# Attention: the turning of the probabilities in two 64-row halves of the array

## The reference

```python
def _sink_attend(q, k, v, mask, sink):
    s = jnp.einsum('bqhgd,bkhd->bhgqk', q, k) * (HEAD_DIM ** -0.5)
    if mask is not None:
        s = jnp.where(mask, s, -jnp.inf)
    m = jnp.maximum(jnp.max(s, axis=-1), sk)          # sk: a logit per head
    p = jnp.exp(s - m[..., None])
    den = jnp.sum(p, axis=-1) + jnp.exp(sk - m)
    o = jnp.einsum('bhgqk,bkhd->bqhgd', p, v)
    return o / den
# latent: blocks of 128 queries; keys are 256 cached ones + a window of 128 before, own 128, 128 after
```

## Time and profile before

| | us |
|---|---|
| median of 3 runs (lowest, highest) | 2705.36 (2704.15, 2711.06) |
| span of the profiled execution (no other time of it is recorded) | 2702.7 |
| attention: from the first scores to the last tile's turning | 173.9 to 1056.5 |
| PE busy over the span | 2641.0 (98%) |
| DVE, ACT, POOL busy | 1248.0 (46%), 870.3 (32%), 641.9 (24%) |
| L1173 (turning), busy on PE | 167.9, 1264 instructions |
| L1190 (values), busy on PE | 168.0, 2528 instructions |

### The profile page before, as it was taken

One profiled execution on the slowest core, in us unless ns is written; L12 is line 12 of the kernel. 1 busy time (PEld: TensorE's weight loads), 2 busy tenths in 40 slices (PEclk: granted clock), 3 DMA queues, 4 the chain that ended last, 5 costly groups with the idle time before them and its releaser, 6 DMA issues.

```text
span 2702.7 us, 47576 instructions
## 1 busy us (share of the span) xinstructions
PE 2641.0 (98%) x17435; PEld 2315.5 (86%) x17435; DVE 1248.0 (46%) x3286; ACT 870.3 (32%) x2222; POOL 641.9 (24%) x833
## 2 busy tenths in 40 slices
PE   5899999999999999999999999999999999999998
PEld 3688888888888887787899999999999999999787
DVE  3656657475665647554234251424233341425533
ACT  3434526353452535222213131222223131313211
POOL 2522031222203121333003030312213040403332
PEclk9999999999999999999999999999999999999999
DMA  9512030211203032443122041313222030315543
GB/s 357 205 49 76 10 95 14 64 56 49 74 12 95 13 93 102 140 135 103 36 36 84 17 83 42 76 42 61 65 38 82 19 108 16 84 43 148 170 140 109
DMA packets 187800, 219.26 MB, mean 81 GB/s; under 512 B 27248, under 2 KB 132480, under 8 KB 185680
## 3 DMA queue, kind: packets, MB, share of 16 engines
q1 hardware_dynamic: 177616, 189.11, 24.8%
q10 hardware_dynamic: 9984, 27.37, 2.6%
HBM read 178.27 MB, written 38.17 MB: 80 GB/s over the span
## 4 chain that ended last, share of the span: by engine, by line
PE 90%; DVE 3%; DMA 2%; issue 2%; ACT 1%; POOL 1%; SPq 0%; ACTq 0%; DVEq 0%; POOLq 0%
PE psum L521 18%; PE psum L523 17%; PE psum L522 17%; PE psum L1190 5%; PE psum L1173 5%; PE psum L1157 2%; PE psum L1160 2%; PE psum L2390 2%; PE psum L2455 2%; PE psum L1940 2%; PE psum L1942 2%; PE psum L1941 2%; PE psum L2458 2%; PE psum L1475 2%; PE psum L1476 2%; PE psum L1477 2%
## 5 line engine op out<-in xcount | busy, mean ns | idle before, releaser
L521 PE MATMUL psum<-h_hi,m_w_lo 128*128 128x384 f32 (+1 forms) x1600 | 594.0, 371 | 1.1 <-ACT gt_nat L1388 1.1
L523 PE MATMUL psum<-h_hi,m_w_hi 128*128 128x384 f32 (+1 forms) x1600 | 573.6, 359 | 0.0
L522 PE MATMUL psum<-h_lo,m_w_hi 128*128 128x384 f32 (+1 forms) x1600 | 573.1, 358 | 0.0
L523 PEld LDWEIGHTS psum<-h_hi,m_w_hi 128*128 128x128 f32 x1600 | 300.5, 188 | 27.0
L521 PEld LDWEIGHTS psum<-h_hi,m_w_lo 128*128 128x128 f32 x1600 | 301.3, 188 | 26.0 <-issue 1.6
L522 PEld LDWEIGHTS psum<-h_lo,m_w_hi 128*128 128x128 f32 x1600 | 301.6, 189 | 22.4
L521 PE MATMUL psum<-h_hi,attn_w_lo 128*128 128x384 f32 (+1 forms) x800 | 291.7, 365 | 0.9 <-DVE attn_w_lo L506 0.6
L523 PE MATMUL psum<-h_hi,attn_w_hi 128*128 128x384 f32 (+1 forms) x800 | 285.8, 357 | 0.0
L522 PE MATMUL psum<-h_lo,attn_w_hi 128*128 128x384 f32 (+1 forms) x800 | 285.5, 357 | 0.0
L881 ACT ACTIVATE arena<-arena,stats 128x640 f32<-128x640 f32 (+2 forms) x272 | 216.1, 795 | 143.3 <-DVE stats L964 143.3
L964 DVE CUSTOM_DVE_ANT_0 arena<-psum,wmask,stats 128x640 f32<-128x640 f32 (+2 forms) x256 | 206.1, 840 | 56.7 <-PE psum L1160 52.9
(11 more groups left out here) (318 smaller groups left out, 4671.9 us busy)
## 6 DMA issues: line engine op xcount, KB each, us to landing
m_bc<-gate_rows_mlstm SPq DMA_DIRECT2D x128, 256.0 KB, 3.4
m_w_raw<-in_mlstm_w_in SPq DMA_DIRECT2D x40, 512.0 KB, 4.7
h_full<-gated_output SPq DMA_DIRECT2D x29, 512.0 KB, 4.1
gated_output<-gT SPq DMA_DIRECT2D x8, 1088.0 KB, 5.2
layer_output<-xb_out ACTq DMA_DIRECT2D x17, 512.0 KB, 2.7
h_hi_full<-layer_output SPq DMA_DIRECT2D x17, 512.0 KB, 4.8
out<-h_hi_full ACTq DMA_DIRECT2D x17, 512.0 KB, 5.0
xb<-in_x_sample ACTq DMA_DIRECT2D x16, 512.0 KB, 7.0
```

The source lines that it names most:

```text
L521: pe.matmul(out, self.lo[:, k, :], E.h_hi[:, k, tok], start=(k == 0), stop=False)
L522: pe.matmul(out, self.hi[:, k, :], E.h_lo[:, k, tok], start=False, stop=False)
L523: ins = pe.matmul(out, self.hi[:, k, :], E.h_hi[:, k, tok], start=False, stop=(k == KT - 1))
```

## The change

The transposes are cut by query rows. Each 128x128 tile becomes two of 64 rows by 128 columns, each against a 64x64 identity, one in rows 0 to 63 of the array and one in rows 64 to 127. The ten tiles of a block (five of each head, in one row of slots, head 0 first) lie in three banks: slots 0 to 7 have their lower query half in bank 4 and the upper in bank 5, and slots 8 and 9 have both halves in bank 7. The upper halves are taken in another order (slots 8 and 9 first), so that both halves of the array are never in bank 7 together; a new semaphore `s_upper` guards that. ACT copies slots 0 to 7 from banks 4 and 5 in one instruction of 1024 columns, DVE copies slots 8 and 9 (256 columns) from bank 7, and only for blocks of five tiles. `s_pT` is raised once by two, after the last transpose. `turn` waits once, ahead of its first transpose, for the exponentials of both heads. ACT's copy of block 1 has a new wait for the gate projection's banks, since the buffer is shared with it.

The copy after the two scans has half the columns. The diff:

```diff
--- before.py
+++ after.py
@@ -553,8 +553,8 @@
         shuf = spare[:, 5, 0:512]
         flat = spare[:, :, :].rearrange("p a n -> p (a n)")
         prob = [flat[:, 5 * D + 512 + b * 640:5 * D + 512 + (b + 1) * 640] for b in range(4)]
-        probT = [sb(f"probT{b}", [P, 2, 5, P]) for b in range(2)]
-        gth = [probT[1][:, :, :, :].rearrange("p h t q -> p (h t q)")[:, e * 512:(e + 1) * 512] for e in range(2)]
+        probT = [sb(f"probT{b}", [P, 10, P]) for b in range(2)]
+        gth = [probT[1][:, :, :].rearrange("p t q -> p (t q)")[:, e * 512:(e + 1) * 512] for e in range(2)]
         k_hi = sb("k_hi", [P, KREQ], F32R)
         sink = sb("sink", [P, NHEAD])
         stats = sb("stats", [P, 6, 2, 2])
@@ -562,7 +562,7 @@
         rden = sb("rden", [P, 4, 2, 4])
         rspr = sb("rspr", [P, 2, HD])
         rturned = sb("rturned", [8, P])
-        kvout = probT[0][:, 0, 0, :].rearrange("p (a d) -> p a d", a=2)
+        kvout = probT[0][:, 0, :].rearrange("p (a d) -> p a d", a=2)
 
         J = Projection(E, ctx, "attn", 5, E.first_w)
         s_cs = [sem(f"rotary_loaded{b}") for b in range(2)]
@@ -581,6 +581,7 @@
 
 
 
+        s_upper = sem("upper_halves_of_last_tiles")
         s_rq, s_rt, s_rw, s_rb, s_scaled = (sem(x) for x in (
             "recip_turned", "recip_copied", "recip_stored", "recip_rows_loaded", "o_scaled"))
         NU = 2 * NT
@@ -610,6 +611,20 @@
             if b == CTX:
                 return [VT_REQ]
             return [0, 1] + [VT_LAT + b + x for x in (-1, 0, 1) if 0 <= b + x < NS]
+
+        PAIRED = 8
+        LONG = NS - 2
+
+        def long_before(b):
+
+            return min(max(b - 1, 0), LONG)
+
+        def turned_half(slot, half):
+
+            if slot < PAIRED:
+                return E.bank[4 + half][:, slot * HD:(slot + 1) * HD]
+            at0 = (slot - PAIRED) * P + half * HD
+            return E.bank[7][:, at0:at0 + HD]
 
         def scores_of(w):
 
@@ -860,18 +875,16 @@
                             act.wait_ge(s_sarg, at(bbase + b + 1))
                             act.activation(esink[:, b % 2, :], sarg[:, b % 2, :], ACT.Exp).then_inc(s_es, 1)
 
-                        def turned_second(b):
+                        def turned_pairs(b):
                             act.wait_ge(s_pT, at(base + 2 * b + 2))
                             if b == 0 and sub == 0:
                                 act.wait_ge(s_kvst, at(kv * 32 + 32))
+                            if b == 1:
+                                act.wait_ge(s_release, at(kv * NB + NG * (3 + 2 * sub)))
                             act.wait_ge(s_pv, at(bbase + (b - 1 if b >= 2 else 0)))
-                            n = min(4, len(value_tiles(b)))
-                            ins = act.copy(probT[b % 2][:, 1, 0:n, :],
-                                           E.bank[5][:, 0:n * P].rearrange("p (t q) -> p t q", t=n))
-                            if len(value_tiles(b)) == 5:
-                                ins = act.copy(probT[b % 2][:, :, 4, :],
-                                               E.bank[7][:, 0:2 * P].rearrange("p (h q) -> p h q", h=2))
-                            ins.then_inc(s_pTB, 1)
+                            n = min(PAIRED, 2 * len(value_tiles(b)))
+                            act.copy(probT[b % 2][:, 0:n, :].rearrange("p t (a q) -> p t a q", a=2),
+                                     E.PS[:, 4:6, 0:n * HD].rearrange("p a (t q) -> p t a q", q=HD)).then_inc(s_pTB, 1)
 
                         def exponential(b, hh):
                             w = 2 * b + hh
@@ -903,7 +916,7 @@
                                 act.copy(E.w_hi[:, 1, :], spare[:, 1, :]).then_inc(s_ewhi, 1)
                             if 2 <= s < NT:
                                 exponential(s, 0)
-                            turned_second(s - 1)
+                            turned_pairs(s - 1)
                             if 2 <= s < NT:
                                 exponential(s, 1)
                                 sink_exp(s)
@@ -966,14 +979,13 @@
                                                      op0=ALU.add, op1=ALU.min,
                                                      accum_out=negm[:, b % 2, hh:hh + 1]).then_inc(s_nm, 1)
 
-                        def turned_first(b):
-                            dve.wait_ge(s_pT, at(base + 2 * b + 1))
+                        def turned_rest(b):
+                            if len(value_tiles(b)) < 5:
+                                return
+                            dve.wait_ge(s_pT, at(base + 2 * b + 2))
                             dve.wait_ge(s_pv, at(bbase + (b - 1 if b >= 2 else 0)))
-                            if b == 0 and sub == 0:
-                                dve.wait_ge(s_kvst, at(kv * 32 + 32))
-                            n = min(4, len(value_tiles(b)))
-                            dve.tensor_copy(probT[b % 2][:, 0, 0:n, :],
-                                            E.bank[4][:, 0:n * P].rearrange("p (t q) -> p t q", t=n)).then_inc(s_pTA, 1)
+                            dve.tensor_copy(probT[b % 2][:, PAIRED:10, :],
+                                            E.bank[7][:, 0:2 * P].rearrange("p (t q) -> p t q", t=2)).then_inc(s_pTA, 1)
 
                         def denominators(b):
                             p = b % 2
@@ -1066,7 +1078,7 @@
                                 softmax_max(2 * s)
                                 softmax_max(2 * s + 1)
                             if s < NT + 1:
-                                turned_first(s - 1)
+                                turned_rest(s - 1)
                                 denominators(s - 1)
                             if s >= 2:
                                 gate(s - 2)
@@ -1100,7 +1112,7 @@
                         if g == 0 and sub == 0:
                             pe.wait_ge(s_vS, at(kv * 3 + 3))
                         elif g == 0:
-                            pe.wait_ge(s_pTA, at(kv * (2 * NT) + NT))
+                            pe.wait_ge(s_pTA, at(kv * (2 * LONG) + LONG))
                             pe.wait_ge(s_pTB, at(kv * (2 * NT) + NT))
                         elif g == 2 and sub == 0:
                             pe.wait_ge(s_kvo, at(kv * 2 + 2))
@@ -1120,7 +1132,7 @@
                         pe.wait_ge(S.s_hd, NT)
                     pe.wait_ge(s_release, at(kv * NB + NG))
                     pe.wait_ge(s_og, at(kv * (2 * NT)))
-                    pe.wait_ge(s_pTA, at(kv * (2 * NT)))
+                    pe.wait_ge(s_pTA, at(kv * (2 * LONG)))
                     pe.wait_ge(s_pTB, at(kv * (2 * NT)))
                     settle(E, pe)
                     for r, (a, z) in enumerate(VGROUPS):
@@ -1163,15 +1175,22 @@
                                     ins.then_inc(s_S, 1)
 
                     def turn(b):
-                        pe.wait_ge(s_pTA, at(bbase + b))
+                        pe.wait_ge(s_pTA, at((kv * 2 + sub) * LONG + long_before(b)))
                         pe.wait_ge(s_pTB, at(bbase + b))
-                        for hh in range(2):
-                            w = 2 * b + hh
-                            pe.wait_ge(s_p, at(base + w + 1))
-                            for t in range(len(value_tiles(b))):
-                                out = E.bank[4 + hh][:, t * P:(t + 1) * P] if t < 4 else E.bank[7][:, hh * P:(hh + 1) * P]
-                                ins = pe.transpose(out, prob[w % 4][:, t * P:(t + 1) * P], E.ident[:, :])
-                            ins.then_inc(s_pT, 1)
+                        n = len(value_tiles(b))
+                        tiles = [(hh, t) for hh in range(2) for t in range(n)]
+                        low, high = tiles, tiles[PAIRED:] + tiles[:PAIRED]
+                        pe.wait_ge(s_p, at(base + 2 * b + 2))
+                        for i, pair in enumerate(zip(low, high)):
+                            if i == PAIRED:
+                                pe.wait_ge(s_upper, at((kv * 2 + sub) * LONG + long_before(b + 1)))
+                            for half, (hh, t) in enumerate(pair):
+                                r = slice(half * HD, half * HD + HD)
+                                ins = pe.transpose(turned_half(hh * n + t, half), prob[(2 * b + hh) % 4][r, t * P:(t + 1) * P],
+                                                   E.ident[r, r])
+                            if n == 5 and i == 1:
+                                ins.then_inc(s_upper, 1)
+                        ins.then_inc(s_pT, 2)
 
                     def pv(b):
 
@@ -1182,12 +1201,12 @@
                         if b >= LONE:
                             pe.wait_ge(s_rs, at((kv * 2 + sub) * (NT - LONE) + b - LONE + 1))
                             pe.transpose(spread, rspr[:, :, :].rearrange("p h d -> p (h d)"), E.ident[:, :])
-                        pe.wait_ge(s_pTA, at(bbase + b + 1))
+                        pe.wait_ge(s_pTA, at((kv * 2 + sub) * LONG + long_before(b + 1)))
                         pe.wait_ge(s_pTB, at(bbase + b + 1))
```

(2 more changed lines are left out.)

## The result

The changed kernel takes 2711.01 us (median of 14 runs, 2707.15 to 2714.24) against 2704.93 for the kernel before (14 runs, 2701.41 to 2711.06): ratio 1.0019, 95% interval 1.0012 to 1.0027. That is within the 0.3% that I had called no change, and within the range, but on the other side: 6 us slower where 6 us faster was forecast.

What follows compares the result with a forecast made beforehand. PE, 99.9% busy in attention, was taken as the bound, with the chain through ACT next. Start -0.6, rounds -0.8, small transposes -0.2, POOL +0.8 made -0.8 a pass, -6.4 in eight: 2705.4 to 2699 us, range 2688 to 2714.

Steps and rivals of the forecast that it cites:

- The turning: PE's transposes in a block: pairs of half transposes run side by side, 0.76 us up to the values instead of 1.24.
- Rival (b): Transposes on PE: the two halves do not run side by side, turning 1.40 us, total 2736, slower; chance 13%.
- What is late next: After PE's saving, scans limit a block to about 3.13 us; the chain through ACT takes 6.99 for two blocks against 7.12.
- (c): Rival: ACT's 1024-column copy over two banks costs 1.05 us or above, +11 over the main case, 2710; chance 10%.
- The sum for a pass: The three engine lists stepped forward through one pass: -0.8 us a pass, -6.4 over eight passes.
- Twelve blocks in the chain: Attention blocks bound by the ACT chain: six two-block rounds of -0.13 us each, -0.8 a pass.
- The end, with its short blocks: End of a pass: no gain, as ACT's 1024-column copy, +0.4 us, gives back what PE saves.
- The 0.07: Time in us to wake PE after the second exponential, an estimate between 0.04 and 0.1.
- The small transposes: Small transposes in eight blocks, 0.1 us each, on the chain only in every other one: -0.2 a pass.
- The start: Start of a pass: first turning loses 0.35 us and the next block 0.25 by the scans' limit, -0.6.
- The POOL term: POOL's gate scaling delays DVE's denominator and the next scan, reaching the chain in two blocks: +0.8 us a pass.

Runs made afterwards that it cites:

- the first experiment: The kernel before with the merged wait alone: PE waits for both heads' exponentials ahead of the first whole transpose; 2724.42 us, ratio 1.0070.

## Why the prediction was wrong

*The turning*: right. 0.76 to 0.78 measured for 0.76, and the order of the halves alone moves 0.41. Rival (b) fell. (The recorded (1.27 - 0.22) / 16 is 0.066 and not 0.064; that moves the turning by 0.01.) By the rule that I quoted of the Trainium skill ("TensorE: Matmul & The Clock Gate", LDWEIGHTS: 128 columns 107 ns, whatever the rows) even ten pairs would take 1.07, an estimate from that page; this trace has twenty loads of 64 rows in 0.83.

*What is late next*: right. The chain over two blocks has the links that I named, PE idles ahead of the turning, released by ACT, in both blocks of this round (0.45 and 0.34), elsewhere 0.8 in every other one, and the clock stayed. Intervals between scores alternate between 3.13 and 3.97 up to POOL's scaling and are 3.6 and 3.5 behind it. PE's busy share fell to 93.8% in the window shown and not below 90%, since that window holds projection too; from 433 to 479, in the chain alone, it is 41.10 of 46.00 us, 89%. The copy at 0.89 for 0.87 leaves (c) out. That the chain and not PE is the bound is shown three ways: 0.43 more on ACT in a round costs 25 us here, all that it can, and in the kernel before a third of what it could; 0.42 less of copy gives 14; half of the turning moved ahead of the second exponential gives 17.5.

*The sum for a pass*: here it failed, in "Twelve blocks in the chain are six rounds of -0.13: -0.8" and in "The end, with its short blocks, gains nothing". The round is 7.11, not 6.99: 0.07 of waking, 0.02 of copy, 0.02 of turning and 0.01 of the scan's start were missing, and these small sizes are the whole gain. The 0.07 was a guess between 0.04 and 0.1 for a wake of PE; it is 0.14. PE never waits in the attention loop of the kernel before, but elsewhere in its trace it does, as here behind DVE:

```profile
369.29 1.39 DVE L506 TENSOR_TENSOR attn_w_lo<-attn_w_raw,attn_w_hi 128x512 fp32r<-128x512 f32 x1 [0.81 <-ACT attn_w_hi L500]
```

```profile
370.83 0.47 PE L521 MATMUL psum<-h_hi,attn_w_lo 128*128 128x512 f32 x1 [0.20 <-DVE attn_w_lo L506]
```

370.83 - (369.29 + 1.39) = 0.15. Other waits of PE in that trace end with 0.05, so the guess should have gone up to 0.15. With 0.15 in place of 0.07 the rounds would have been worth -0.3 instead of -0.8 a pass, and the forecast about -2 us. The small transposes gave nothing either. The start gave what it should: the second interval of the pass fell from 6.34 to 5.99 and the third from 3.34 to 3.14, -0.55. The end I had taken as even: a copy of +0.4 against PE's saving. But the copy is not on its path; PE stands at the exponentials of block 15, and the lone tile of block 16 costs 0.22 more as halves.

Where the end's loss comes from shows in the two kernels with POOL's scaling short, since there the alternation runs through to the end of the pass. Between them the six rounds differ by +0.05 in all, the last interval by 4.16 - 3.50 = +0.66, and the stretch to the next pass by +0.06: twelve intervals are six rounds, but there is a thirteenth, it is a long one again, and I had no term for it. With the scaling the same +0.7 stands as 0.2 in the last interval (3.50 to 3.70) and 0.5 behind it (44.10 to 44.60). The POOL term I had as +0.8; those two kernels say +0.1 to +0.2. So per pass: -0.55 at the start, 0 for -1.0 in the rounds, +0.7 for 0 at the end, +0.2 for +0.8 from POOL: +0.35, measured 0.31 to 0.44, where I had -0.8. That the time fell inside the range was luck: terms wrong by +1.0 and +0.7 a pass, 14 us in all, hid behind one wrong by -0.6, 5 us; with the POOL term alone put right the forecast would have been further off.

*What stays open*: of the 6.1 us between the medians attention holds 3.0. The rest lies outside it, where nothing of the work was changed. In the profiles the start of attention varies by 5.7 us with the clock granted in the first 110 us: the time at the lower level there runs from about 7 us (attention begins at 173.7) to 27 (at 179.4). The mean granted clock is on record for every run of the experiments and for the changed kernel's own: 0.9938 in the mean of 70 runs of kernels with halves, 0.9947 in 84 of kernels with whole transposes, so the kernels with halves do meet the lower level a little more. Why is open. Among the 57 later runs of the kernel before, 0.001 of clock goes with 1.3 us, so of the 3 us outside attention this is about 1; the changed kernel and the one before differ by 2.2 to 4.8 us between runs of the same recorded clock, which is about what attention holds. The medians minus attention of the variants scatter by -1.6 to +3.9 about those of the kernel before. Also open is why PE wakes 0.14 to 0.15 after the exponential ahead of the turning but 0.05 after it in the middle of it.

The deeper reason is in the first experiment: with the merged wait already there, the array halves are worth 13 us (2724.4 to 2711.0; 17 in attention, the dearer copy included), and the merged wait had spent 18 to 20. The change is both at once, and its two parts nearly cancel.

## What to carry to other kernels

When two parts of a step are interleaved so that they share a wait, price the wait first: list what stands behind it up to the next turn of the loop, and compare that chain with the engine's own work. If the difference is below the sum of the small guesses (wakes, copies over a new shape), the forecast is "no change", whatever the engine saves. Then look for the order that keeps the early half of the work ahead of the late wait; here that was worth 20 us, and moving a copy to the idler engine another 8. Count the intervals that the chain holds as well: where a chain makes long and short blocks in turn, an odd number of them ends on a long one.

## Not expected of the hardware

Twenty half-array transposes take 0.83 where they alternate between the halves and 1.24 where one half follows the other: the order of issue decides whether the halves overlap. A lone pair of tiles turned in halves between matmuls of the full array cost 0.59 in place of 0.37, so changing from whole to half of the array and back seems to have a price of about 0.1 each way (argued from this place, not tried by itself). DVE's subtraction of the low weights took 1.48 instead of 0.68 while POOL worked for 1.28 on its scaling, yet with the scaling nearly gone a pass was only 0.3 to 0.4 shorter: a stretched operation beside a chain costs what sticks out of its slack.
